# Two-layer diffusion backbone with routed experts: the rows of the first expert step made by one-hot products, the overflow loop in turns of six blocks, and constant products where TensorE waits

## What is computed

```python
def hier_moe(h, wg, bg, we, be, w1, w3, w2):
    g_logits = h @ wg + bg                              # 4 groups
    _, g_sel = lax.top_k(g_logits, 1)
    p_group = take_along_axis(softmax(g_logits), g_sel)
    e_logits = (h @ we + be).reshape(N, 4, 8)[g_sel]    # 8 experts of the chosen group
    top_p, top_i = lax.top_k(softmax(e_logits), 2)
    weights = p_group * top_p / sum(top_p)
    expert = g_sel * 8 + top_i
    # for each token: sum over its 2 experts of weight * (silu(h @ w1[e]) * (h @ w3[e])) @ w2[e]

h_lat = layer_norm(ALPHA * h_lat + m[2] * mixer(modulate(h_lat, m[0], m[1])))
h_lat = layer_norm(ALPHA * h_lat + m[5] * hier_moe(modulate(h_lat, m[3], m[4])))
```

## Time and profile before

| | us |
|---|---|
| median of 3 runs | 2463.87 (2461.80 to 2465.14) |
| the profiled execution | 2463.27 |
| its span, first to last instruction | 2461.4 |
| TensorE matmul busy | 2313.6 (94%) |
| DVE / ACT / POOL busy | 768.4 / 418.8 / 280.7 |
| mean granted TensorE clock | 0.972 |
| hidden values L1091 (largest two groups) | 524.9 + 163.2 |
| memory traffic, mean over the span | 232 GB/s |

### The profile page before, as it was taken

One profiled execution on the slowest core, in us unless ns is written; L12 is line 12 of the kernel. 1 busy time (PEld: TensorE's weight loads), 2 busy tenths in 40 slices (PEclk: granted clock), 3 DMA queues, 4 the chain that ended last, 5 costly groups with the idle time before them and its releaser, 6 DMA issues.

```text
span 2461.4 us, 28375 instructions
## 1 busy us (share of the span) xinstructions
PE 2313.6 (94%) x10444; PEld 1164.1 (47%) x10444; DVE 768.4 (31%) x1753; ACT 418.8 (17%) x912; POOL 280.7 (11%) x341
## 2 busy tenths in 40 slices
PE   6989999999996999999998999999996999999987
PEld 3546547888554344443333444444553444443332
DVE  3694114555537111111113511111345111111115
ACT  1301233444121101110102200000111101110111
POOL 0000103223122100000000000000232000000000
PEclk9999999999997999999999999999996999999999
DMA  9881000000316999999897210102207999999986
GB/s 386 297 349 58 0 1 1 2 19 19 125 55 257 387 419 414 418 413 409 357 418 278 87 51 26 51 26 88 91 35 298 419 419 416 419 407 410 374 346 256
DMA packets 146797, 572.28 MB, mean 232 GB/s; under 512 B 25033, under 2 KB 50793, under 8 KB 103914
## 3 DMA queue, kind: packets, MB, share of 16 engines
q1 hardware_dynamic: 133418, 536.97, 55.1%
q0 software_dynamic: 13248, 33.57, 3.6%
HBM read 549.51 MB, written 35.65 MB: 238 GB/s over the span
## 4 chain that ended last, share of the span: by engine, by line
PE 81%; DMA 7%; DVE 6%; SPq 2%; issue 2%; POOL 1%; ACT 1%; DVEq 0%; POOLq 0%; ACTq 0%
PE bank L1091 23%; PE bank L1165 13%; PE bank L1113 11%; PE bank L707 8%; PE bank L1014 4%; PE bank L974 4%; PE bank L664 3%; PE bank L810 3%; DVE lnwb L1525 2%; DMA bigA<-in_moe_w 2%; PE bank L1194 2%; SPq L445 2%; PE bank L824 1%; PE bank L793 1%; DMA bigC<-in_moe_w 1%
## 5 line engine op out<-in xcount | busy, mean ns | idle before, releaser
L1091 PE MATMUL bank<-bigA,bigB 128*32 128x512 f32 (+2 forms) x2048 | 524.9, 596 | 0.0
L1165 PE MATMUL bank<-bigB,bigA 128*128 128x512 f32 x768 | 331.6, 595 | 2.0 <-ACT bigB L1244 2.0
L1091 PEld LDWEIGHTS bank<-bigA,bigB 128*32 128x32 f32 (+2 forms) x2048 | 187.1, 141 | 299.1 <-issue 297.0
L707 PE MATMUL bank<-bigC,bigB 128*128 128x512 f32 (+3 forms) x768 | 292.4, 536 | 0.0
L1113 PE MATMUL bank<-bigA,bigB 128*32 128x512 f32 (+2 forms) x992 | 259.2, 612 | 14.8 <-DMA bigA<-in_moe_w 11.8
L1165 PEld LDWEIGHTS bank<-bigB,bigA 128*128 128x128 f32 x768 | 146.5, 191 | 186.6 <-issue 186.6
L707 PEld LDWEIGHTS bank<-bigC,bigB 128*128 128x128 f32 x768 | 142.4, 192 | 127.6 <-issue 119.5
L1244 ACT ACTIVATE bigB<-bank,small 128x128 f32<-128x128 f32 x288 | 107.5, 460 | 381.7 <-PE bank L664 381.7
L1091 PE MATMUL bank<-bigC,bigB 128*32 128x512 f32 (+2 forms) x640 | 163.2, 594 | 0.0
L1113 PEld LDWEIGHTS bank<-bigA,bigB 128*32 128x32 f32 (+2 forms) x992 | 91.4, 143 | 142.3 <-issue 138.2
L2150 POOL DMA_INDIRECT y_rows<-bigB,ints x44 | 44.5, 1011 | 909.0 <-DVE bigB L1936 909.0
(11 more groups left out here) (286 smaller groups left out, 2279.7 us busy)
## 6 DMA issues: line engine op xcount, KB each, us to landing
bigA<-in_moe_w SPq DMA_DIRECT2D x292, 1024.0 KB, 20.6
bigC<-in_moe_w SPq DMA_DIRECT2D x92, 1024.0 KB, 22.9
bigA<-in_ada_w SPq DMA_DIRECT2D x40, 1024.0 KB, 7.4
bigA<-y_rows SPq DMA_DIRECT2D x16, 1024.0 KB, 4.9
bigA<-in_w_in_odd SPq DMA_DIRECT2D x24, 512.0 KB, 6.2
bigA<-in_ada_w SPq DMA_DIRECT2D x4, 2048.0 KB, 12.5
bigC<-in_w_in_even SPq DMA_DIRECT2D x4, 2048.0 KB, 14.3
h_rows<-bigC SPq DMA_DIRECT2D x16, 512.0 KB, 4.8
```

Source lines behind the costliest of these rows:

```text
L707: last = mm(bank(n % 3)[:, 0:w], uT[:, k, t * P:(t + 1) * P], wring[:, g % 2, k, at_:at_ + w], start=(k == 0), stop=(k == KC - 1))
L1091: last = mm(bank(m)[at_:at_ + w, :], xT[:, j, KC // 2 * h + k, at_:at_ + w], w13_at(SLOT_OF[m, h, q][0], k), start=(h == 0 and k == 0), st ...
L1165: last = mm(bank(3 * half + m), wc[:, j, m, k, :], u1T[:, k, half * 512:(half + 1) * 512], start=(k == 0), stop=(k == KC - 1))
```

## The change

Four parts, and the semaphore counts that go with them.

1. **Rows of block 0.** DVE compares each row's rank within experts 0 and 1 with the lanes 1 to 64 and so has eight one-hot tiles (`first_is`, 128x1024 in one instruction). TensorE multiplies the rows that are in SBUF (`hh`) with them: 8 column groups x 8 tiles, 64 products of 128x128, which give block 0's rows already transposed. POOL gathers no rows for block 0. The rank products stand ahead of the counts; the 16 products of the table move from ahead of the blocks to between the two halves of block 0's hidden values; block 0's output is finished before block 1 begins. The copy of `order` by DVE stands ahead of the 16 pairs of one-hot tiles. SP's piece 12 also waits for the 64 products (they read `hh`), and the wait for a gather stands at piece 16 in place of piece 14, and is for block 1's.
2. **Overflow.** A turn has six blocks, so the loop has 4 turns in place of 12. The count is read earlier. SP issues the loads of the last step's first residual rows ahead of the loop, two quarters of a block's hidden values before the end.
3. **Last step.** The two diagonals for `gate_rows` are built in the last block in place of behind the loop; the first `gate_rows` stands ahead of `combined(0)`; the load of the first pair is in two halves by column, and the second half of `combined(0)` waits for the second.
4. **Constant products** (`fill`): "ones" times 512 columns of constants, into banks that nobody reads: 2 and 1 in `last_rows` (layer 0 and 1), 6, 1 and 1 in `moe`, 2 and 1 around the last `stream_T` of layer 0.

```diff
+OVER, OVER_TURN = 24, 6
-            with eng.Fori(0, OVER // 2) as i:
-                with eng.If(2 * i < n_over):
-                    for j in range(2):
-                        block_(i + NB // 2, j)
+            with eng.Fori(0, OVER // OVER_TURN) as i:
+                with eng.If(OVER_TURN * i < n_over):
+                    for j in range(OVER_TURN):
+                        block_(OVER_TURN // 2 * i + NB // 2 + j // 2, j % 2)
...
                 if n == PREFETCH:
-                    sp.wait_ge(S("routed"), 6 * l + 4)
+                    sp.wait_ge(S("routed"), 7 * l + 5)
                     sp.wait_ge(S("h_out"), 16 * NT * (l + 1))
-                if n == PREFETCH + 2:
-                    sp.wait_ge(S(f"xg_in{l}_0"), 16)
+                    sp.wait_ge(S(f"x_T{l}"), 1)
+                if n == PREFETCH + 4:
+                    sp.wait_ge(S(f"xg_in{l}_1"), 16)
...
-                sp.wait_ge(S(f"h_mm{l}"), 4 * NB)
-                sp.wait_ge(S(f"y_mm{l}"), NB)
+                sp.wait_ge(S(f"h_mm{l}"), 4 * NB - 2)
                 for t in range(2):
                     load(hback[:, t], h_dram[l][t * P:(t + 1) * P, :], f"x_in{t}")
...
+                    if t == 0:
+                        load(pair[:, 0, :, 0:512], rows[:, :, 0:512], "pair_in0")
+                        load(pair[:, 0, :, 512:], rows[:, :, 512:], "x_in2")
+                    else:
+                        load(pair[:, t % 2], rows, f"pair_in{t % 2}")
...
+            def fill(b, n):
+                for _ in range(n):
+                    mm(bank(b), cc("ones"), cst[:, 0:512], start=True, stop=True, skip_group_check=True)
...
+                pe.wait_ge(S("res"), l * NT + NT - 1)
+                fill(0, 2)
                 rows_T(l, NT - 1)
+                fill(0, 1)
                 logits(l, NT - 1)
...
+                fill(0, 6)
+                pe.wait_ge(S("routed"), 7 * l + 1)
                 rank = bank(2)[:, 0:NT * NE]
...
+                fill(0, 1)
+                pe.wait_ge(S("routed"), 7 * l + 2)
+                for k in range(KC):
+                    for t in range(NT):
+                        if k == 0:
+                            pe.wait_ge(S("ln"), 2 * l * NT + t + 1)
+                        last = mm(bank(6 + k // 4)[:, (k % 4) * P:(k % 4 + 1) * P], cols(hh[:, t])[:, k, :], first_is[:, t, :],
+                                  start=(t == 0), stop=(t == NT - 1), skip_group_check=True)
...
-                gathered_T(0, 0, 1)
-                gathered_T(1, 1, 1, 6)
-                for b in range(NB):
+                fill(0, 1)
+                hidden_half(0, 0)
+                table()
+                hidden_half(0, 1)
+                gated_T(0)
+                output(0)
+                n_over = over_count(pe, l)
+                for b in range(1, NB):
...
             moe(0)
             for t in range(2):
                 residual_part(0, t)
+            gate_rows(2, diag1[:, 0], 2)
             for t in range(NT):
                 combined(0, t)
-                if t < 2:
-                    gate_rows(t + 2, diag1[:, t], (2, 6)[t])
+                if t == 0:
+                    gate_rows(3, diag1[:, 1], 6)
                 if t:
                     stream_T(t - 1)
+            fill(4, 2)
             stream_T(NT - 1)
+            fill(4, 1)
...
+                rank = bank(2)[:, 0:256].rearrange("p (t e) -> p t e", t=NT)
+                V(v.scalar_tensor_tensor(first_key.rearrange("p (t e) -> p t e", t=NT), rank[:, :, 0:2], 1.0,
+                                         chosen.rearrange("p (t e) -> p t e", t=NT)[:, :, 0:2], ADD, MUL))
+                V.wait()
+                v.tensor_tensor(first_is[:, :, :].rearrange("p t (e s) -> p (t e) s", e=2),
+                                wide(cc("iota")[:, 1:65].unsqueeze(1), [P, 2 * NT, 64]),
+                                wide(first_key.unsqueeze(2), [P, 2 * NT, 64]), ALU.is_equal).then_inc(S("routed"), 1)
...
+                act.wait_ge(S("route_mm"), 8 * l + 5)
+                modulated(parts(xT[:, 0]), 6, mod_of(l, 1), f"xT_ev{l}")
+                act.wait_ge(S(f"x_T{l}"), 1)
+                modulated(parts(xT[:, 0]), 6, mod_of(l, 1), f"xT_ev{l}", 4, KC)
...
-                gather(0, tok[:, 0:1])
                 gather(1, tok[:, 1:2])
+                gather(0, tok[:, 2:3])
```

More of the change, by code:

```diff
@@ L624, in _ @@
                         sp.wait_ge(S("comb"), l * NT + t - 1)
-                    load(pair[:, t % 2], y_dram[l][t * 2 * P:(t + 1) * 2 * P, :].rearrange("(p k) n -> p k n", k=2),
-                         f"pair_in{t % 2}")
+                    rows = y_dram[l][t * 2 * P:(t + 1) * 2 * P, :].rearrange("(p k) n -> p k n", k=2)
+                    if t == 0:
[3 more added lines that the diff above has]
+                        load(pair[:, t % 2], rows, f"pair_in{t % 2}")
                     if t >= 2:
@@ L1064, in moe @@
-                for c in range(16):
-                    pe.wait_ge(S("spot"), l * 16 + c + 1)
-                    last = mm(bank(1)[:, 0:TABLE], lane_is[:, c, :], step_is[:, c, :], start=(c == 0), stop=(c == 15))
-                last.then_inc(S("route_mm"), 1)
+                mm(bank(3)[:, 0:NE], cc("ones"), ahead[:, NT, :], start=True, stop=True, skip_group_check=True)
+                mm(bank(3)[0:NE, NE:NE + 4], ahead[:, NT, :], cc("ones")[:, 0:4], start=True, stop=True,
+                   skip_group_check=True).then_inc(S("route_mm"), 1)
@@ new lines, in moe @@
+                fill(0, 1)
[6 more added lines that the diff above has]
+                                  start=(t == 0), stop=(t == NT - 1), skip_group_check=True)
+                    if k == 3:
+                        last.then_inc(S("route_mm"), 1)
+                    if k == 4:
+                        pe.wait_ge(S("routed"), 7 * l + 3)
+                        mm(bank(4)[:, 0:3 * NE], cc("ones")[0:NE, :], rows4[:, 0:3 * NE], start=True, stop=True)\
+                            .then_inc(S("route_mm"), 1)
@@ new lines, in moe, with table @@
+                last.then_inc(S(f"x_T{l}"), 1)
+                pe.wait_ge(S("routed"), 7 * l + 4)
+                mm(bank(5)[0:1, 0:NE], cc("expert")[0:NE, :], re32[2][0:NE, :], start=True, stop=True, skip_group_check=True)
+                mm(bank(5)[0:1, NE:2 * NE], cc("ones")[0:NE, 0:1], rows4[:, 3 * NE:], start=True, stop=True,
+                   skip_group_check=True).then_inc(S("route_mm"), 1)
+                def table():
+                    for c in range(16):
+                        pe.wait_ge(S("spot"), l * 16 + c + 1)
+                        last = mm(bank(4)[:, 0:TABLE], lane_is[:, c, :], step_is[:, c, :], start=(c == 0), stop=(c == 15))
+                    last.then_inc(S("route_mm"), 1)
@@ L1192, in combined @@
                 for n in range(2):
+                    if t == 0 and n:
+                        pe.wait_ge(S("x_in2"), 48 + 16 * (l + 1))
                     for k in range(2):
@@ L1882, in moe @@
                 V.wait()
+                dve.wait_ge(S("route_mm"), 8 * l + 7)
+                incl = re32[0]
+                V(v.tensor_copy(incl[0:1, :], bank(5)[0:1, NE:2 * NE]))
+                v.tensor_copy(order[0:1, :], bank(5)[0:1, 0:NE]).then_inc(S("routed"), 1)
                 for c in range(16):
@@ L1943, in scattered @@
                     output(b % 2)
-                rows_T(0, 0)
-                rows_T(1, 1, 6, "u_ev_d")
-                for b in range(NB):
-                    if b:
+                gate_up(0)
+                gated(0)
+                rows_T(1, 1)
+                scattered(0)
+                n_over = over_count(dve, l)
+                for b in range(1, NB):
+                    if b >= 2:
                         gated(b - 1)
                     gate_up(b)
-                    if b:
-                        rows_T(b + 1, (b + 1) % 2)
+                    rows_T(b + 1, (b + 1) % 2)
+                    if l == 0 and b == NB - 1:
+                        gate_diag(diag1[:, 0], 4 + 2)
+                        gate_diag(diag1[:, 1], 4 + 5)
+                    if b >= 2:
                         scattered(b - 1)
```

123 lines of the change are left out of this document (55 added, 68 removed).

## The result

| | before | after |
|---|---|---|
| median, us | 2462.84 (4 runs) | 2494.04 (2491.62 to 2496.53, 4 runs) |
| ratio, 95% interval | | 1.0127 [1.0109, 1.0144] |
| span of the profiled execution | 2461.4 | 2493.1 |
| TensorE busy | 2313.6 | 2381.9 |
| mean granted clock | 0.972 | 0.988 |

The forecast was 2453.8, with 2440 to 2462 as its range; the kernel is 31 us slower than before. TensorE's clock went up, its busy time as well, and the time with them.

The account below looks back on a forecast made before the run. Experts were taken as bound by the full stream of pieces, gains possible only where TensorE waits or is slow. -6.7 - 2.4 - 3.3 + 1.1 + 1.2 = -10.1 on 2463.27; median 0.6 higher: 2453.8, range 2440 to 2462.

Parts of the forecast that it names:

- The step that failed: Routing, block 0's one-hot products: 128 counts at 0.11 us, 14.1 us in all; 17.3 at 0.135.
- What bounds the kernel: Experts: the stream of 1 MB pieces has no slack, so a head start of TensorE is given back at 930.86.
- this wait, at 796.1: Routing: piece 12 waits for the 64 products and `order`, going out at 796.1 in place of 794.76.
- the 6 us of waiting: Sign in the experts: TensorE waits about 6 us at the piece it meets at 930.86.
- How the stream is delayed: Experts: piece 16 waits for block 1's gather, goes at 813.9, 1.1 us later; +1.1 and +1.2 by layer.
- R2: Rival: routing or its gather 3 us later than thought in each layer, passed on by the stream: 2459.8; chance 0.18.
- the forecast's bound of +4.2 us a layer: Upper bound of the stream's delay, with products at 0.135 us or a gather of 7.60 us.
- R1: Rival: TensorE's head start in the experts comes through, 4.9 us per layer gained: 2441.7; chance 0.17.
- The last steps: Overflow loop and last step: -6.7 us in layer 0, -3.3 in layer 1, by an earlier pair loaded in halves.
- the 6 that I had named as a sign of being wrong: Sign: the prediction is wrong if the last steps together gain less than 6 us.
- The fills: Constant products raise TensorE's clock: -0.7 us before routing; -0.7 and -1.7, -2.4 in all, at layer 0's end.
- -0.7 at the start: Before the routing: fills of `last_rows` keep TensorE busy, so eight transposes run at the higher clock, -0.7 us.

Follow-up runs that it names:

- e2: Changed kernel, but the 64 products read 128 neighbouring columns of `hh` in place of every eighth (rows permuted): 2462.44 us, ratio 0.9996 to the kernel before.
- e6: Changed kernel with piece 16's wait for block 1's gather taken off: 2481.11 us, ratio 1.0077 to the kernel before.
- e9: e5 with pieces 12 to 15 each waiting only for the products of the tiles in their slot: 2450.68 us, ratio 0.9946 to the kernel before.
- e11: e1 with piece 12 held until TensorE has done block 0's first quarter: 2472.73 us, ratio 1.0040 to the kernel before.
- e5: Changed kernel with 16 products of 512 columns, operands exchanged, and no gather wait at piece 16: 2448.68 us, ratio 0.9945 to the kernel before.
- e13: Changed kernel with the products' stationary columns 16 bytes apart in place of 32; permuted rows made layer 1 overflow: 2729.77 us.
- e7: e1 without any constant products (empty `fill`): 2462.71 us, ratio 1.0000 to the kernel before.
- e1: Changed kernel with part 1 alone undone, block 0's rows gathered again: 2458.34 us, ratio 0.9977 to the kernel before.
- e8: e1 with the last step's first pair as one load of 1 MB: 2458.66 us, ratio 0.9981 to the kernel before.

## Why the prediction was wrong

**The step that failed** is "the 64 products count as 128 ... 0.11 each: 14.1 us", with 0.135 as its other end. It was 0.24, outside both. The 0.11 was taken from transposes, another instruction, and the 0.135 from products of neighbouring columns. The code said `cols(hh[:, t])[:, k, :]`, every eighth column, and I never asked of a product whether its operands were read so. The shape was the same, the access wasn't. e2 shows it alone: 15.5 us with neighbouring columns, and 32 us of the kernel's time. Why the transposes, those of the earlier trace rows even from the same `hh`, read columns as far apart at 0.11 is open; it wasn't tried.

**What bounds the kernel** was right, that the experts' end follows the stream, and it is why the error cost its full size. Products that take 16.7 us longer than thought, started 2 us earlier, hold back TensorE, but 11 us of that were in hand, since I had block 0 start so much earlier than before. What they held back besides was the stream: piece 12 waits for them, since they read `hh` in its slot. The forecast had this wait, at 796.1, and passed on all that came later "one to one"; e2 has piece 12 at 796.8 and the experts' end at +2.7 where I had +1.1. One reading under it was too strong: at 930.86, where I had TensorE at the landing of a piece, it had stood still for 0.1 us, and for 0.25 at 2013.75. The stream and TensorE were level there; in layer 0 of the kernel before the first wait for a piece of over 2 us is the 4.5 us at 1183.7. Nor did the 6 us of waiting come at this one product: the changed kernel waited 4.4 us at 915.29 and 0.5 at 947.73.

**How the stream is delayed** I had only half. I put it on the issue of piece 16, and e6, e9 and e11 show that it is the bytes: the DMA engines' idle time before they are full for good, as long as there are slots. So R2's "3 us late" was the right kind of case with a fifth of its size, and the forecast's bound of +4.2 us a layer had the products at 0.135 at most.

**R1** (the head start comes through) is wrong for this kernel: the start was 10.4 us early in e2 and the end 2.7 late. It became right in part in e5, where the stream was let go with TensorE: piece 16 was 9.7 us early there and the end 3.1.

**The last steps** were over-sized. The loop's turns stayed at 0.76 us and the scatter's landing bound, at 3.35 us: both as forecast. The pair's first half landed in 4.2 us, not 3.0, and its second half was there 8.2 us after the pair's issue, not 5.1. Sharing the engines with the next pair doesn't explain that by itself, since the whole pair of before shared them too and took 4.74; it stays open. So layer 0's last step and the mixer behind it gained 5.3 us and not 9.8 (2.8 to 7.6 in the other traces with parts 2 to 4). In layer 1 the last step gained nothing in the changed kernel's one profile (+0.4), and 0.3 to 3.1 in those of the experiments other than e13, against my -3.3. The working in the prediction also takes 1.4 us for the second half of `combined(0)` in layer 0, where four counts at its own 0.46 are 1.8. Together the last steps gained 4.9 us, under the 6 that I had named as a sign of being wrong.

**The fills** were right. The convolution's first products run at a granted 1.00 where the earlier trace rows has 0.50, eight counts in 3.38 us in place of four, and e7 puts all fills at 4 us. Their -0.7 at the start is not told apart: layer 0's routing begins at 774.6 to 777.1 in the traces with fills and at 776.8 to 777.9 in those without, so most of the changed kernel's -3.3 there is not shown to come from the change.

## What to carry to other kernels

Price a product by how its operands are read, not by its shape alone: in the 128x128 products here 32-bit columns 32 bytes apart doubled the time in either operand, and 16 bytes apart did in the stationary one, while 8 bytes apart did not. Where the DMA engines are full for a long stretch, count the bytes that are in at its start: (lost GB/s x window) / full rate gave the shift of layer 0's end within 1.4 us in eight kernels, and neither a head start of TensorE nor the issue of one transfer did. And a buffer that is still read is a transfer not yet sent; what reads it should be short, or be split so that its parts come free, if there are free slots behind them.

## What was not expected of the hardware

The price of distant columns in a product (0.24 us a count against 0.12), with transposes at 0.11 from columns as far apart. One branch of 3.4 to 3.9 us in a loop of four turns that jump over six blocks, where the same branch took at most 0.7 in twelve turns over two blocks. And two halves of a transfer of 1 MB that were complete 7.3 to 8.2 us after the first was issued (e1, the changed kernel), where the whole took 4.7 to 4.9 (before, e8).
